# One pass for overflowing experts, a later bias, and w_down in two runs: a mixture-of-experts kernel with 32 streamed experts

## The reference

```python
logits = h @ w_router + b_router            # 32 experts
top_v, top_e = lax.top_k(logits, 4)
gate = softmax(top_v)
# for every expert e, for the tokens that chose it:
gu  = xb @ w_gate_up[e] + b_gate_up[e]      # (1024, 2048)
g, lin = gu[:, :1024], gu[:, 1024:]
g   = minimum(g, 7);  lin = clip(lin, -7, 7)
act = g * sigmoid(1.702 * g) * (lin + 1)
y   = act @ w_down[e] + b_down[e]           # (1024, 1024)
out[t] = sum over the 4 chosen experts of gate * y
```

## Time and profile before

| | |
|---|---|
| time, median of 3 runs | 1128.84 us (1127.72 to 1129.25) |
| the profiled execution's own time | 1128.84 us |
| its span from first to last instruction | 1127.1 us |
| mean granted TensorE clock | 0.990 |
| PE busy | 1079.8 us, 96% of the span |
| PEld busy | 483.2 us, 43% |
| DVE, ACT, POOL busy | 25%, 16%, 7% |
| DMA, mean over the span | 384 GB/s, q1 in use 92.0% |
| instruction fetches on q8 | 34 packets, 0.56 MB |

### The profile page before, as it was taken

The page is one execution under the profiler, slowest core; times in us unless marked ns, Lnnn a source line. Parts: engine busy times, 40 slices in busy tenths (PEclk is TensorE's granted clock), DMA queues, the critical chain, the costliest instruction groups (busy, mean ns, idle before and its releaser), DMA issues.

```text
span 1127.1 us, 14049 instructions
## 1 busy us (share of the span) xinstructions
PE 1079.8 (96%) x5847; PEld 483.2 (43%) x5848; DVE 284.7 (25%) x661; ACT 175.3 (16%) x303; POOL 75.2 (7%) x153
## 2 busy tenths in 40 slices
PE   7999999989999999999999999999999999999996
PEld 6888775433333433333333333333333333333332
DVE  6999752211111111111111111111111111111112
ACT  3111402211111111111111111111111111111112
POOL 3975000000000000000000000000000000000000
PEclk9999999999989999999999999999999999999998
DMA  7853588899998999999999999999999999999993
GB/s 231 270 175 122 211 351 328 341 371 423 422 416 358 419 429 428 435 430 435 430 428 435 434 431 430 428 437 433 431 429 428 437 433 431 429 430 430 420 421 138
DMA packets 42616, 432.27 MB, mean 384 GB/s; under 512 B 5599, under 2 KB 21389, under 8 KB 24556
## 3 DMA queue, kind: packets, MB, share of 16 engines
q1 hardware_dynamic: 42572, 431.64, 92.0%
HBM read 430.58 MB, written 1.05 MB: 383 GB/s over the span
## 4 chain that ended last, share of the span: by engine, by line
PE 79%; DVE 10%; DMA 5%; issue 2%; ACT 2%; another core or an unknown queue 1%; SPq 1%; DVEq 0%
PE bank L1453 38%; PE bank L1465 19%; DVE bank L907 6%; PE bank L1474 5%; PE bank L1411 5%; DMA ring<-w_gate_up 4%; PE bank L1424 3%; PE bank L1376 2%; PE bank L1341 2%; ACT area L696 2%; PE bank L1445 1%; PE bank L1429 1%; DVE bank L942 1%; DMA ring<-ssm_b_im 1%
## 5 line engine op out<-in xcount | busy, mean ns | idle before, releaser
L1453 PE MATMUL bank<-ring,area 128*64 128x512 f32 x2048 | 450.3, 596 | 10.8 <-DMA ring<-w_gate_up 10.8
L1453 PEld LDWEIGHTS bank<-ring,area 128*64 128x64 f32 x2048 | 156.3, 138 | 288.8 <-issue 262.3
L1465 PE MATMUL bank<-ring,area 128*64 128x512 f32 x1024 | 228.4, 598 | 4.1 <-ACT area L696 2.2
L1073 DVE TENSOR_SCALAR area<-bank 128x512 f32<-128x512 f32 x32 | 22.1, 691 | 748.5 <-PE bank L1453 748.5
L1465 PEld LDWEIGHTS bank<-ring,area 128*64 128x64 f32 x1024 | 72.1, 138 | 140.0 <-issue 133.7
L1230 PE MATMUL bank<-area,ring 128*128 128x256 f32 x480 | 106.6, 381 | 2.1 <-DVE area L829 1.2
L1230 PEld LDWEIGHTS bank<-area,ring 128*128 128x128 f32 x480 | 90.3, 190 | 16.9 <-DMA ring<-w_in 2.5
L702 ACT ACTIVATE area<-area 128x512 f32<-128x512 f32 x32 | 20.1, 630 | 473.2 <-DVE area L1073 473.2
L907 DVE SCALAR_TENSOR_TENSOR bank<-ring,spread,bank 128x256 f32<-128x256 f32 x174 | 71.5, 482 | 0.6
L1474 PE MATMUL bank<-area,spT 64*128 64x512 f32 x248 | 62.9, 626 | 2.0 <-issue 2.0
L1411 PE MATMUL bank<-rows,pick 128*64 128x512 f32 x256 | 62.0, 604 | 0.4 <-DVE onehot L1062 0.4
(11 more groups left out here) (245 smaller groups left out, 541.3 us busy)
## 6 DMA issues: line engine op xcount, KB each, us to landing
ring<-w_gate_up SPq DMA_DIRECT2D x49, 4096.0 KB, 37.4
ring<-w_down SPq DMA_DIRECT2D x26, 4096.0 KB, 34.0
ring<-w_gate_up SPq DMA_DIRECT2D x16, 2048.0 KB, 16.9
ring<-w_gate_up SPq DMA_DIRECT2D x28, 1024.0 KB, 11.5
ring<-w_down SPq DMA_DIRECT2D x18, 1024.0 KB, 20.6
ring<-w_in SPq DMA_DIRECT2D x15, 1024.0 KB, 8.1
ring<-w_down SPq DMA_DIRECT2D x3, 2048.0 KB, 11.2
ring<-w_out SPq DMA_DIRECT2D x1, 4096.0 KB, 14.0
```

Of the source, the lines that this page charges most:

```text
L1453: last = mm(bank[4 + b][64 * h:64 * h + 64, :], heT[:, k % 4, k // 4 * 64:k // 4 * 64 + 64], w[:, b * FF + h * 512:b * FF + h * 512 + 512] ...
L1465: last = mm(bank[b][64 * h:64 * h + 64, :], src[:, k, :], w[:, k % 2, h * 512:h * 512 + 512], start=(k == 0), stop=(k == KD - 1))
```

## The change

1. `more_blocks` stands once on each engine, behind expert 15 (MID = 16), as a loop over all 32 experts under `if any_more > 0`. As the ring then holds other experts' weights, that pass loads its own and afterwards restores those of expert 16. The ordinary experts have no branch behind them. `more_done` is gone from SP.
2. `down_bias` moves on PE from behind expert 3 to just before that pass, behind expert 15.
3. w_down's rows lie otherwise: partition p holds rows 4p to 4p+3 of each half of the matrix. A load of four slots reads two runs of 16 KB for each partition, where it read one of 32 KB; loads of one and two slots still read one run of 8 or 16 KB.
4. The activations are turned by four 128x128 transposes (`transposes(gc, 4)`) in place of the 32 records of 64x64. DVE's `times_sigmoid` writes them in the new order.
5. `turn_act` transposes the spread matrix before it waits for `act_ready`.
6. END has sizes for two more experts: 27 and 28 get (4, 2, 2, 4) and semaphores of their own, where they had (4, 4, 4); expert 29 goes from (4, 2, 2, 4) to (4, 2, 1, 1, 4). On PE experts 26 to 29 are written out as well, the loops being 4 to 15 and 16 to 25.

```diff
-END = {E - 3: (4, 2, 2, 4), E - 2: (4, 2, 1, 1, 1, 1, 1, 1), E - 1: (2, 2, 2, 1, 1, 1, 1, 1, 1)}
+END = {E - 5: (4, 2, 2, 4), E - 4: (4, 2, 2, 4), E - 3: (4, 2, 1, 1, 4),
+       E - 2: (4, 2, 1, 1, 1, 1, 1, 1), E - 1: (2, 2, 2, 1, 1, 1, 1, 1, 1)}
+MID = 16
...
-        dn_v = w_down[0].rearrange("e (p k) n -> e p k n", p=128)
+        dn_v = w_down[0].rearrange("e (h p m) n -> e h p m n", p=128, m=4)
...
+                elif n == 4:
+                    src, dst = dn_v[e].rearrange("h p m n -> p h m n"), grid(room, 2, 4, D)
                 else:
-                    src, dst = dn_v[e, :, 2 * c:2 * c + 2 * n, :], grid(room, 2 * n, D)
+                    src, dst = dn_v[e, c // 2, :, c % 2 * 2:c % 2 * 2 + 2 * n, :], grid(room, 2 * n, D)
...
             def refill(e, half, parts):
 
-                more_done(e)
...
             def times_sigmoid():
-                return v.tensor_tensor(gc.rearrange("a (k p) -> a p k", k=KD), grid(lc, 64, KD), grid(sg, 64, KD), ALU.mult)
+                return v.tensor_tensor(gc.rearrange("a (m p) -> a p m", p=128), grid(lc, 128, 4), grid(sg, 128, 4), ALU.mult)
...
-            def act_transposes():
-                for k in range(KD):
-                    for h in range(2):
-                        r, c = slice(64 * h, 64 * h + 64), slice(k * 64, k * 64 + 64)
-                        last = mm(bank[4][r, c], gc[r, c], ident[r, r], start=True, stop=True)
-                return last
...
                     for h in range(2):
-                        last = mm(bank[b][64 * h:64 * h + 64, :], src[:, k, :],
+                        last = mm(bank[b][64 * h:64 * h + 64, :], src[:, k % 4, k // 4 * 64:k // 4 * 64 + 64],
                                   w[:, k % 2, h * 512:h * 512 + 512], start=(k == 0), stop=(k == KD - 1))
...
                 pe.wait_ge(spread_ready, e + 1)
+                spread_transposes().then_inc(spT_pe, 1)
                 pe.wait_ge(act_ready, e + 1)
-                spread_transposes().then_inc(spT_pe, 1)
-                act_transposes().then_inc(aT_pe, 1)
+                transposes(gc, 4).then_inc(aT_pe, 1)
...
             def expert(e, half, uses):
 
                 gates_up(e, half, uses)
                 add_last(e)
                 fetch_next(e)
                 downs(e, half, uses)
-                more_blocks(e, half, e + 1)
 
             expert(1, 1, first_loads)
             for e in range(2, len(EARLY)):
                 expert(e, e % 2, [first_loads[g] + 16 * loads_of(e - 2, g) for g in range(3)])
+            with pe.Fori(len(EARLY) // 2, MID // 2) as i:
+                for half in range(2):
+                    expert(i * 2 + half, half, [i * 16 + n for n in later(half)])
             pe.wait_ge(down_in, 32)
             for n in range(4):
                 down_bias(n)
-            with pe.Fori(len(EARLY) // 2, E // 2 - 2) as i:
+            more_blocks()
+            with pe.Fori(MID // 2, E // 2 - 3) as i:
                 for half in range(2):
-                    expert(i * 2 + half, half, [i * 16 + n for n in later[half]])
-            expert(E - 4, 0, [(E // 2 - 2) * 16 + n for n in later[0]])
-            expert(E - 3, 1, E - 3)
+                    expert(i * 2 + half, half, [i * 16 + n for n in later(half)])
+            expert(E - 6, 0, [(E // 2 - 3) * 16 + n for n in later(0)])
+            for e in range(E - 5, E - 2):
+                expert(e, e % 2, e)
...
-            more_blocks(E - 2, 0, E)
-            more_blocks(E - 1, 1, E)
             pe.wait_ge(y_row, E)
```

More of the change, by code:

```diff
@@ L322, in build, with loads_of, later @@
         gu_v = w_gate_up[0].rearrange("e (p k) n -> e p k n", p=128)
-        dn_v = w_down[0].rearrange("e (p k) n -> e p k n", p=128)
+        dn_v = w_down[0].rearrange("e (h p m) n -> e h p m n", p=128, m=4)
+        first_loads = 64, 64, 64
+        def loads_of(e, g):
+            ends = itertools.accumulate(EARLY[e])
+            return sum(1 for n in ends if 4 * g < n <= 4 * g + 4)
+        def later(half):
+            return [first_loads[g] + 16 * (loads_of(half, g) + loads_of(half + 2, g) - 2) for g in range(3)]
         @block.sync
@@ L734, in root_table, with more_blocks @@
                 s.activation(neg_top, ident[:, 0:2], ACT.Sqrt)
-            def more_blocks(e, end=False):
+            def more_blocks():
                 with act.If(any_more > 0):
[L739 to L744, removed]
-                            h_row_copy().then_inc(step, 1)
[L746 to L763, removed]
@@ L773, in _, with expert @@
+            def expert(e):
+                activate(e)
+                copy_next(e)
+                act.wait_ge(chunk_used, e * PER + PER)
+                y_row_copy().then_inc(y_row, 1)
+            with act.Fori(0, MID // 2) as i:
+                for half in range(2):
+                    expert(i * 2 + half)
+            more_blocks()
+            with act.Fori(MID // 2, E // 2 - 1) as i:
+                for half in range(2):
+                    expert(i * 2 + half)
             activate(E - 2)
@@ L1113, in gate_and_lin, with more_blocks @@
                 times_sigmoid().then_inc(act_ready, 1)
-            def more_blocks(e, half):
+            def more_blocks():
                 with dve.If(any_more > 0):
[L1118 to L1139, removed]
@@ L1148, in _, with expert @@
+            def expert(e, half):
+                pick_next(e, half)
+                dve.wait_ge(chunk_used, e * PER + KD)
+                gate_and_lin(e)
+            with dve.Fori(0, MID // 2) as i:
+                for half in range(2):
+                    expert(i * 2 + half, half)
+            more_blocks()
+            with dve.Fori(MID // 2, E // 2 - 1) as i:
+                for half in range(2):
+                    expert(i * 2 + half, half)
             pick_next(E - 2, 0)
@@ L1528, in more_blocks @@
                             scatter().then_inc(step, 1)
-                            pe.wait_ge(step, o + 2)
+                            pe.wait_ge(step, a + 2)
                             gather().then_inc(step, 1)
[L1531 to L1535, removed]
@@ L1545, in more_blocks @@
-                        gather().then_inc(step, 1)
-                        pe.wait_ge(step, a + 4)
-                        transposes(hrow, 7).then_inc(step, 1)
-                        pe.wait_ge(step, a + 6)
-                        pe.sem_inc(passed, 1)
-            def loads_of(e, g):
-                ends = itertools.accumulate(EARLY[e])
-                return sum(1 for n in ends if 4 * g < n <= 4 * g + 4)
-            first_loads = 64, 64, 64
-            later = [[first_loads[g] + 16 * (loads_of(half, g) + loads_of(half + 2, g) - 2) for g in range(3)] for half in range(2)]
+                            pe.wait_ge(step, a + 4)
@@ L1572, in _ @@
             downs(0, 0, first_loads)
-            more_blocks(0, 0, 1)
             def expert(e, half, uses):
```

153 lines of the change are left out of this document (102 added, 51 removed).

## The result

| | before | after |
|---|---|---|
| time, median of the runs beside each other | 1128.28 us | 1114.11 us |
| ratio, 95% interval | | 0.9884 [0.9856, 0.9912] |
| profiled execution: own time, span | 1128.84, 1127.1 | 1113.72, 1112.0 |
| last weights land (issue time plus time to landing) | 1108.4 | 1099.1 |
| from there to the end of the span | 18.7 | 12.9 |

The kernel is 1.2% faster, with the forecast of 1117 some 3 us above the time and the range 1112 to 1124 around it. The kernel before scatters more than the changed one: beside e1 to e4 its 13 runs lie between 1121.40 and 1131.33 us with a median of 1125.7, and there the changed kernel (e4) is 12.1 us faster.

What follows compares the result with a forecast made beforehand. The prediction took the weight queue as the bound, with PE's speed counting only at head and tail. Head −8.0, runs and END +2.0, tail −6.2 made −12.2 us: 1116.6, stated as 1117, range 1112 to 1124 for 8 in 10.

Steps and rivals of the forecast that it cites:

- What sets the pace: Middle of the kernel: the one weight queue, 9.71 us for each 4 MB load, sets the pace, not PE.
- The head: Around experts 0 to 4: without pauses and bias, slots free earlier and the queue no longer runs dry, −8.0 us.
- The smaller hole at 240: Queue at 324 GB/s from 235 to 245 us, around the pause behind expert 0: 2.3 us lost.
- The bias in the middle: Behind expert 15: bias, jump and half clock cost PE 13 us at most, covered by the queue, so 0.
- w_down in two runs: 26 four-slot loads of w_down in 16 KB runs take 0.07 us more each: +1.8 us.
- The finer END: Last experts: splitting two w_gate_up groups of 4 MB and one of 2 MB costs +0.2 us.
- Turns: Activation transposes: 0.5 us less for each expert, hidden behind the queue in the middle.
- The tail: After the last weights land: PE ends 2.3 us behind in place of 6.6, shorter pause, faster scatter, −6.2 us.
- A: Rival: only one end, head or tail, gives its gain, 1120 to 1125 us; chance 0.17.
- B: Rival: w_down's two runs cost over 0.54 us more a load, so the kernel gets slower; chance 0.07.
- C: Rival: PE is the bound throughout, so its savings give −23.4 us, 1105; chance 0.01.
- D: Rival: run costs of 0.2 us a load balance the lower bounds of both ends, 1128 us; chance 0.03.

Runs made afterwards that it cites:

- e1: Kernel before with only the down bias moved behind expert 15, branches kept: 1121.01 us, ratio 0.9967.
- e4: The changed kernel run once more, unaltered, as a measure of spread: 1113.64 us, ratio 0.9905.
- e6: Changed kernel with w_down's four-slot loads in eight runs of 4 KB for each partition: 1125.76 us, ratio 0.9988.
- e8: Changed kernel with 96 more matmul records on PE behind the bias in the middle: 1114.04 us, ratio 0.9873.
- e2: Kernel before with all more_blocks calls taken out, bias still behind expert 3: 1112.92 us, ratio 0.9892.
- e9: Kernel before with branches kept, but PE's skipped body cut to one wait and one semaphore step: 1112.99 us, ratio 0.9891.
- e11: Changed kernel with the old END load sizes in the last experts: 1113.51 us, ratio 0.9886.
- e13: Kernel before with short skipped bodies on PE behind experts 0 to 3 only, full bodies behind 4 to 31: 1119.54 us, ratio 0.9958.
- e3: Changed kernel with the down bias put back behind expert 3: 1114.27 us, ratio 0.9906.
- e7: Changed kernel with w_down in one run of 32 KB, w_gate_up's columns read in groups of four: 1112.68 us, ratio 0.9856.
- e12: The kernel of e7 run once more, w_down in one run and four 128x128 turns: 1111.44 us, ratio 0.9873.
- e10: Changed kernel with old 64x64 turns, w_down in one run, spread's transposes behind the wait again: 1113.53 us, ratio 0.9891.

## Why the prediction was right

**What sets the pace.** Right. The share is 1.00 or more in every stretch from 245 to 900, PE waits about where it was forecast (in expert 15, then from 18 on in place of 20, for 25 us in all), and the last weights land at 1099, 3 before the 1102 that was named. The queue at 9.7 us for 4 MB sets the middle: 11 us more of transfers moved the time by 11 (e6), 12.5 us more of PE moved it by nothing (e8).

**The head, −8.0.** Right in place and mechanism, too small: the windows give 11.3 us, 10.2 net of what before had ahead at 235. Up to 4 us of that may be the slow run that the trace of before is; the medians can't part head from tail. The step was mis-sized where it held back 2.2 of the 10.2 for small pieces and instruction fetches, and counted nothing for 245 to 335 us. There the queue made 422 GB/s before and 429 after, with loads cut alike, so the pieces were not what it lost. Nor did most of the fetches stay: of the page's 34 packets 9 fall into this stretch before and 4 after. The runs with 3 or 4 there and no pause made 426 to 430 GB/s (e2, e4, e9 to e11, e13), e1 with 8 and its pauses 425. The bytes of five fetches, 0.08 MB, are far less than the 0.63 MB lost, and no run parts pauses from fetches, so the cause of these 7 GB/s stays open. The smaller hole at 240 is open too, as e4 has it without a pause (365 GB/s) and e2 without bodies (348).

**Which edit does it.** The prediction took out pauses and bias together. The runs part them. The bias at its old place is free once nothing pauses (e3, e9), and 3.63 us long, not 6.59; the half clock then falls behind it, onto expert 4. The body's removal alone gives it all (e2), and on PE alone it is enough (e9). The move of the bias by itself gives part of the head, 4.7 us between medians (e1), as it takes 6.59 out of a stretch that the pauses had made too long.

**The bias in the middle, 0.** Right: 3.90 there and 1.5 of half clock behind it, no pause, and 12.5 us more are still covered (e8).

**w_down in two runs, +1.8.** Right: 9.78 for 9.71, and e7 and e12, with one run, land 2.5 and 3.6 earlier than the changed kernel, the scatter between single traces included. Partitions 16 KB apart and halves 2 MB apart cost no more than these 0.07 us a load.

**The finer END, +0.2 and a paced tail.** Not to be told from nothing (e11). The tail is short without it (e9: 12.9).

**Turns.** Hidden in the middle: right, as PE's waits for w_gate_up rose from 10.8 to 23.6 us. At the end they help by 0.7 in the traces (e12 against e10), which the layout that goes with them takes away.

**The tail, −6.2.** It gave −5.7: −4.0 for the forecast −4.3, −1.3 for −1.2, −0.4 for −0.7. The last one was mis-sized, and not by the clock: the granted clock is 1.00 there, and the first half of the scatter takes 1.15, as it does in e2, e9, e10 and e12. The forecast's 0.9 is about half of the 1.92 that the whole scatter takes without a break before it.

**Luck.** The forecast of 12.2 us was made against a run of 1128.84. Between the two traces the gain is 15.1, between medians it is 14.2 in the first comparison and 12.1 in e4's; how near 12.2 is depends on which runs of before stand beside it. The head gave 2 to 3 us more than was forecast and the tail 0.5 less, so the total hides part of the first.

**The rivals.** A, that only one end gives, was the serious one, as pauses might have stayed with the one body left. None did, at either end, and e13 shows what A would have been: 1119.5, inside its 1120 to 1125 but for half a microsecond. B is nearly what e6 makes: 10.19 for the 9.71 of before is 0.48 a load, 12.5 us, short of its break-even of 0.54; e6 can't be told from the kernel before. C fails on 25 us of waits. D would have needed both lower bounds; neither end was that small.

**What stays open.** Why a jump over a long body stops PE at some places and not at others: behind expert 0 2.38 us, behind 1 and 2 nothing, with the same body. What the traces add: from 400 to 1000 us the trace of before has no packet on the instruction queue q8 and no pause, though the loop jumps over a body behind each of some 20 experts; its pauses stand in code written out or in a loop's first turn, where q8 fetches, and in five of its six pauses a fetch begins within 1.0 us ahead of the pause. Other jumps have a fetch beside them and no pause. Where code lies was not varied by itself.

## What to carry to other kernels

Rarely used work that is skipped by a branch can have a price on TensorE that its own instructions don't show: look for issue time in the chain behind each skipped body, and move long bodies out of line, or once for all, before reordering any work around them. Where one queue feeds the kernel, as here, only two places of PE count: where it must free the first buffers before the queue runs dry, and what is left to do behind the last landing; cost an edit by what it does to the GB/s in the one and to the distance from the last landing in the other. Work that looks slow, as the bias did, may owe part of it to the clock behind a pause. And compare means of instructions over stretches of one granted clock before calling one access pattern slower than another.

## What the runs showed of the hardware

- TensorE pauses 1.3 to 2.9 us at some jumps over a body of some 430 instructions (as counted for e9), and at none over what e9 leaves of it, nor without bodies (e2). It didn't pause at the repeated jumps of a loop (before, 400 to 1000 us). The Trainium skill (Runtime: NRT & Kernel Launch, Instruction fetch mechanics) says that a taken branch out of the pages already fetched stalls until the target page is there; by that rule a short body, whose end is fetched already, costs nothing, and the traces agree (e9). They don't show the pages themselves. The rule's window is two pages of 256 instructions, and there the traces go another way: a turn of before's loop runs 308 matmul records and as many weight loads, over 600 instructions, and nothing was fetched from 400 to 1000 us. The measurement decides.
- The granted clock fell to its half level (1.2 of 2.4 GHz) behind a pause of 2.49 us without the bias (e1, 0.54 from 324.72 to 328.40 us), and behind the bias without a pause (e2, 0.55 from 326.79 to 330.50; also e3, e9 and the changed kernel). With both, 1.77 us of pause and the bias, the eight matmuls of the bias took 6.59 in place of 3.63. Other pauses were not followed by a fall: 2.38 us behind expert 0 and 1.70 at 1060.04.
- By the landings behind 400 us, 4 MB to 128 partitions take 9.71 to 9.72 us in runs of 32 KB, with partitions 32 or 64 KB apart (before, e7, e12), 9.78 in runs of 16 KB and 16 KB apart, and 10.19 in runs of 4 KB and 4 KB apart (e6).
- A moving operand of 128x512 in float32 read in pieces of 16 bytes at equal distances costs nothing that shows: 592.8 ns a record against 592.5, both over records at a granted clock of 1.00 (e7, the changed kernel).
